# Three norms of a two-layer decoder step: GpSimd instead of VectorE adds blocks 2 to 7 to X

## The reference, cut to what matters

```
def rmsnorm(x, w):
    y = x * rsqrt(mean(x * x, axis=-1) + 1e-6)
    return y * w

def ffn_sublayer(x, pre_w, w_gate, w_up, w_down, post_w):
    h = rmsnorm(x, pre_w)
    y = (silu(h @ w_gate) * (h @ w_up)) @ w_down
    return x + rmsnorm(y, post_w)

# layer 0:  x = x + rmsnorm(even_mixer(rmsnorm(x, mix_pre0)), mix_post0);  x = ffn_sublayer(x, ...)
# layer 1:  x = x + rmsnorm(mamba2_mixer(rmsnorm(x, mix_pre1)), mix_post1);  x = ffn_sublayer(x, ...)
```

## Time and profile before

| what | us |
|---|---|
| median of three runs (lowest, highest) | 1102.64 (1100.86, 1103.34) |
| profiled execution, span from its first to its last instruction | 1097.7 |
| between that span and the median of the runs | 4.9 |
| busy in the span: PE / DVE / ACT / POOL | 1031.3 / 705.6 / 503.3 / 52.9 |
| the nine adds of 128x576 at line 2211, together | 6.8 |

### The profile page before, as it was taken

One profiled execution on the slowest core, in us unless ns is written; L12 is line 12 of the kernel. 1 busy time (PEld: TensorE's weight loads), 2 busy tenths in 40 slices (PEclk: granted clock), 3 DMA queues, 4 the chain that ended last, 5 costly groups with the idle time before them and its releaser, 6 DMA issues.

```text
span 1097.7 us, 21745 instructions
## 1 busy us (share of the span) xinstructions
PE 1031.3 (94%) x8763; PEld 947.1 (86%) x8763; DVE 705.6 (64%) x1296; ACT 503.3 (46%) x902; POOL 52.9 (5%) x97
## 2 busy tenths in 40 slices
PE   8999999888889999999889999889999799999996
PEld 7988888533579999999889999768889799999995
DVE  5644678655448566643498997778984676566343
ACT  5222444232355344343458675554764543444341
POOL 8001300000000000000000000021000000000000
PEclk9999999879898999999989999899999899999998
DMA  9637999999953555455524555089135265554501
GB/s 303 185 99 251 331 348 348 339 348 348 338 173 115 161 180 160 150 168 166 171 78 153 170 177 154 1 281 330 45 121 157 81 189 154 176 169 135 182 30 43
DMA packets 193074, 206.17 MB, mean 188 GB/s; under 512 B 7172, under 2 KB 185561, under 8 KB 192923
## 3 DMA queue, kind: packets, MB, share of 16 engines
q1 hardware_dynamic: 174046, 178.65, 51.6%
q10 hardware_dynamic: 15232, 14.68, 4.2%
q0 software_dynamic: 3696, 11.45, 3.3%
HBM read 192.59 MB, written 12.17 MB: 187 GB/s over the span
## 4 chain that ended last, share of the span: by engine, by line
PE 84%; DVE 7%; DMA 3%; ACT 2%; POOL 1%; issue 1%; SPq 1%; ACTq 0%; POOLq 0%; DVEq 0%
PE acc L822 21%; PE acc L824 21%; PE acc L823 21%; PE trb L915 3%; PE scb L936 3%; PE acc L915 3%; PE scb L1048 2%; PE scb L793 1%; DVE RR L1802 1%; DMA ring<-in_state_ssm_dram 1%; DMA ring<-in_cache_v_dram 1%; SPq L597 1%; DVE X L2211 1%; DVE Y L2210 1%; PE acc L1196 1%
## 5 line engine op out<-in xcount | busy, mean ns | idle before, releaser
L822 PE MATMUL acc<-HX,WHL 128*128 128x288 f32 x928 | 281.0, 303 | 14.8 <-DVE HX L1814 10.2
L823 PE MATMUL acc<-HX,WHL 128*128 128x288 f32 x928 | 277.5, 299 | 0.0
L824 PE MATMUL acc<-HX,WHL 128*128 128x288 f32 x928 | 277.1, 299 | 0.0
L1401 ACT ACTIVATE WHL<-ring 128x1024 fp32r<-128x1024 f32 (+1 forms) x140 | 138.8, 1039 | 200.3 <-PE acc L824 200.3
L1825 DVE TENSOR_TENSOR WHL<-ring,WHL 128x1024 fp32r<-128x1024 f32 (+1 forms) x140 | 163.5, 1208 | 69.5 <-ACT WHL L1401 69.4
L822 PEld LDWEIGHTS acc<-HX,WHL 128*128 128x128 f32 x928 | 178.4, 192 | 18.2 <-issue 12.9
L823 PEld LDWEIGHTS acc<-HX,WHL 128*128 128x128 f32 x928 | 179.9, 194 | 0.2
L824 PEld LDWEIGHTS acc<-HX,WHL 128*128 128x128 f32 x928 | 179.4, 193 | 0.0
L1401 ACT ACTIVATE W<-ring 128x1024 fp32r<-128x1024 f32 x84 | 82.6, 1031 | 130.4 <-PE acc L824 130.4
L1825 DVE TENSOR_TENSOR W<-ring,W 128x1024 fp32r<-128x1024 f32 x84 | 97.1, 1197 | 54.1 <-ACT W L1401 54.1
L822 PE MATMUL acc<-HX,W 128*128 128x288 f32 x352 | 105.7, 300 | 5.5 <-DVE HX L1814 5.1
(11 more groups left out here) (413 smaller groups left out, 1855.3 us busy)
## 6 DMA issues: line engine op xcount, KB each, us to landing
ring<-in_l_w_in_dram SPq DMA_DIRECT2D x32, 1024.0 KB, 5.4
ring<-in_l_ffn_gate_dram SPq DMA_DIRECT2D x22, 1024.0 KB, 5.3
ring<-in_l_ffn_up_dram SPq DMA_DIRECT2D x22, 1024.0 KB, 5.3
ring<-in_l_ffn_down_dram SPq DMA_DIRECT2D x16, 1024.0 KB, 5.1
Z<-in_cache_k_dram SPq DMA_DIRECT2D x52, 256.0 KB, 7.7
ring<-in_cache_k_dram SPq DMA_DIRECT2D x52, 256.0 KB, 7.3
Z<-in_cache_v_dram SPq DMA_DIRECT2D x48, 256.0 KB, 7.1
ring<-in_cache_v_dram SPq DMA_DIRECT2D x48, 256.0 KB, 6.6
```

The costliest lines, as they stand in the source:

```text
L822: pe.matmul(out, w[:, 0, at:at + P], part_at(k, 0), start=(k == 0), stop=False)
L823: pe.matmul(out, w[:, 0, at:at + P], part_at(k, 1), start=False, stop=False)
L824: last = pe.matmul(out, w[:, 1, at:at + P], part_at(k, 0), start=False, stop=(k == kdim - 1))
L1401: act.activation(split_weights(i)[:, 0, half], ring[:, slot_of(u), half], ACT.Copy).then_inc(w_hi, 1)
```

## The change

At the three norms ahead of a projection DVE goes on with multiplying all of Y by RR, and with adding blocks 0 and 1 to X. Blocks 2 to 7 are added by POOL, in three instructions of two blocks each. DVE counts up `y_scaled` when a pair is multiplied, POOL waits for that and counts up `x_later` when a pair is added, and ACT waits for `x_later` before it scales a block from 2 on. DVE doesn't wait behind these multiplies any more. At the last norm everything stays with DVE. The nine adds stand in POOL's program at two places: six behind the stores of the conv rows, three behind the stores of the states.

```
+            def add_later(n):
+                for i, first in enumerate((2, 4, 6)):
+                    pool.wait_ge(y_scaled, 3 * n + i + 1)
+                    pool.tensor_tensor(X[:, first:first + 2, :], X[:, first:first + 2, :], Y[:, first:first + 2, :],
+                                       ALU.add).then_inc(x_later, 1)
...
+            add_later(0)
+            add_later(1)
             pool.wait_ge(acc_full, ACC_SSD)
...
+            add_later(2)
             pool.wait_ge(stored, 16 * stores[0])
...
-            def pre_norm(i, hx, col, x_base):
+            def pre_norm(i, hx, col, n):
                 for k in range(KD):
-                    act.wait_ge(x_made, x_base + k + 1)
+                    if k < 2:
+                        act.wait_ge(x_made, 2 * n + k + 1)
+                    else:
+                        act.wait_ge(x_later, 3 * n + k // 2)
                     scaled(hx, k, col + k)
...
-                    link(dve.tensor_tensor(y, y, RR[:, :].unsqueeze(1).to_broadcast([P, size, NT]), ALU.mult))
-                    dve.tensor_tensor(x, x, y, ALU.add).then_inc(x_made, size)
+                    ins = dve.tensor_tensor(y, y, RR[:, :].unsqueeze(1).to_broadcast([P, size, NT]), ALU.mult)
+                    if hx is not None and first >= 2:
+                        ins.then_inc(y_scaled, 1)
+                    else:
+                        link(ins)
+                        dve.tensor_tensor(x, x, y, ALU.add).then_inc(x_made, size)
```

More of the change, by code:

```diff
@@ L336, in hybrid_decoder_kernel @@
         x_made = sem("x_made")
+        y_scaled = sem("y_scaled")
+        x_later = sem("x_later")
         qz_made = sem("qz_made")
@@ L1353, in _ @@
             for i in range(2):
-                pe.wait_ge(x_made, 3 * KD + 4 * i + 4)
+                pe.wait_ge(x_made, 3 * 2 + 4 * i + 4)
                 for t in range(3):
@@ L1612, in _ @@
             post_norm(N_DOWN0, ACC_DOWN0, 3, PN["ffn_post0"], 1)
-            pre_norm(N_IN1, HX1, PN["mix_pre1"], KD)
+            pre_norm(N_IN1, HX1, PN["mix_pre1"], 1)
             def dt_function(step, dst, src, func, scale=1.0):
@@ L1759, in _ @@
             post_norm(N_OUT1, ACC_OUT1, CX // KD, PN["mix_post1"], 2, input_norm=True)
-            pre_norm(N_GU1, HX2, PN["ffn_pre1"], 2 * KD)
+            pre_norm(N_GU1, HX2, PN["ffn_pre1"], 2)
             hiddens(1, N_GU1, ACC_GU1)
```

## The result

The changed kernel takes 1109.11 us in the median of five runs (1102.23 to 1110.82); the kernel before, run beside it, 1101.61 (1100.25 to 1103.34). The ratio is 1.0068, with a 95% interval of 1.0042 to 1.0093: slower by 7.5 us, where 3.7 were forecast. The profiled execution's span is 1108.3 us against 1097.7. That pair lies further apart than the medians: nearly every timed execution takes 1.7 us more than its own span, so the profiled one of the kernel before took about 1099.4 (an estimate from 1097.7 and 1.7), some 3 us less than its median of 1102.64. Most of the 4.9 us that the table of before puts outside the span is this scatter.

The account below looks back on a forecast made before the run. PE carries 84% of the chain, waiting on DVE at the norms. Losses of 0.55, 1.68 and 1.45 us make 3.7, added to the median 1102.64 for 1106.3 us; range 1101.0 to 1109.5.

Parts of the forecast that it names:

- The two engines take turns: At the norms, DVE and POOL reads of SBUF exclude each other; 3.7 us slower; chance 0.42 with a near 1.2.
- The price of an add, a = 1.2: Each POOL add of two blocks at the norms takes 1.2 us, against 0.76 on DVE; ends 0.76 and 2.03.
- the midway value: a = 1.2 us per POOL add, midway between 0.85 for one stream of 576 and 1.56 for two.
- near 1.2 us of work: Sign of being right: POOL's nine adds at the three norms each show near 1.2 us of work.
- Who comes first: At the norms POOL starts only where DVE has nothing lined up; first add behind the multiply of 4-5, 330.35 to 331.55.
- 1.93: Lateness of DVE's row at a norm in us, L = 3a - 1.67, from three handovers and three slower adds.
- From lateness to PE: At the three norms, DVE lateness beyond the spare time costs PE: 0.55, 1.68 and 1.45 us, together 3.7.
- spare time of 1.38, 0.25 and 0.48: DVE lateness in us that costs PE nothing at the first, second and third norm; all beyond it costs.
- The clock at the norms: Rival: without turns, PE's clock rises sooner at the first two norms, 1 us won each, 1099.4 us; chance 0.10.
- the case without turns: Rival: POOL reads while DVE works at the norms without slowing; together -1.2 us, 1101.4 us; chance 0.24.
- The sum: Losses at the three norms, 0.55, 1.68 and 1.45 us, together 3.7 us, giving 1106.3 us.
- the dearest adds: POOL adds at the norms at a = 1.56 give 1109.5 us, at 2.03 1113.8; later clock or beyond 1.56: chance 0.11.

Follow-up runs that it names:

- writes alone: Kernel before, DVE adding all blocks, with POOL writing a scratch tile three times without reading after each pair at the norms: 1100.87 us, ratio 1.0009.
- dead adds: Kernel before, DVE adding all blocks, with POOL adding 512 columns of a constant into a scratch tile after each pair at the norms: 1109.27 us, ratio 1.0082.
- the last batch: Kernel before and changed kernel, each with about half the first PE fill plus 6 products, beside the kernel before (1099.85 us): 1098.51 and 1099.13 us.
- changed, filled: Changed kernel with 68 small dead products on PE ahead of four waits of the state stage: 1106.67 us, ratio 1.0060 to the kernel before.
- before, half the fill: Kernel before with 5, 14, 4 and 10 dead PE products in the state stage, 6 more ahead of the samples' own scores: 1098.51 us, ratio 0.9980.

## Why the prediction was right in its direction, and where not

*The two engines take turns: right.* POOL's and DVE's reads exclude each other, and DVE's row ends later though it has less to do. Held instructions on DVE in a kernel where no work at the norms waits for POOL show it (1.59 for 0.75), writes alone do not.

*The price of an add, a = 1.2: right, in part by luck.* Freed of its wait it is 1.27 to 1.28; the midway value had no row of an add behind it. "GPSIMD Engine Reference" of the Trainium skill, section on elementwise cycle accounting, had led to an estimate of 1.27, and the trace agrees. The profile's mean of 1.69 is add and wait together, as the first norm's rows show; I had named "near 1.2 us of work" as the mark, and who takes 1.69 for the work would call the step wrong.

*Who comes first: wrong, and this is the step that failed in the norms.* I let POOL start only where DVE had nothing lined up, from one old place (a select of 3.83 us). POOL takes its turn at the end of a DVE instruction, mostly the next one. At the third norm the multiply of 4-5 did come first, as I had it:

```profile
876.80 0.51 DVE L1829 SCALAR_TENSOR_TENSOR HX<-X,par,HX 128x288 fp32r<-128x288 f32 x1
877.23 0.75 DVE L2225 TENSOR_TENSOR Y<-Y,RR 128x576 f32<-128x576 f32 x1
879.86 1.50 DVE L1829 SCALAR_TENSOR_TENSOR HX<-X,par,HX 128x288 fp32r<-128x288 f32 x2 [1.88 <-ACT HX L1404]
881.28 0.75 DVE L2225 TENSOR_TENSOR Y<-Y,RR 128x576 f32<-128x576 f32 x1
881.95 2.11 DVE L1829 SCALAR_TENSOR_TENSOR HX<-X,par,HX 128x288 fp32r<-128x288 f32 x2
```

Blocks 2 and 3 were then late as computed (the rest of block 3 ends 7.39 us behind the first multiply; I had 7.43). But the third add did not wait for the row of multiply and rests to end: it went between the rests of 4 and 5, which is why two of them took 2.11. So the splits were 1.41 to 1.48 us late, not 1.93. In the first norm the earlier turn showed on PE as well: I had its block 2 start 0.84 us later than before, and it starts 0.43 sooner, 3.40 us behind PE's first product instead of 3.83.

```profile
331.08 0.40 PE L834 MATMUL acc<-HX,WHL 128*128 128x288 f32 x1 [0.23 <-DVE HX L1829]
```

*From lateness to PE: right in form.* Less the spare time of 1.38, 0.25 and 0.48, that lateness gives 0.03, 1.16 and 1.00; measured 0.26, 1.08 and 1.23. In the second norm DVE no longer waits for the root, as forecast. PE waited for the sum at all three norms, also at the second, where I had named no such wait: it comes for the sum 15.98 and 15.95 us behind the first multiply in the first two norms, hardly sooner than before (16.05 and 15.97), and the sum is 1.41 late against 1.38 and 1.30 to spare.

*The clock at the norms: a rival had it.* I had tied a sooner rise to the case without turns. It came with turns: from PE's first product on, over the same 7.70 us as in the earlier trace rows, the mean is 0.81 instead of 0.50. This is a tendency, not a rule: over the same 7.70 us the 16 changed norms of the kept profiles have 0.60 to 0.81, but for one of 0.50, and 23 unchanged ones 0.50 to 0.62, but for three of 0.75 to 0.78 (those beside dead adds left out).

```profile
327.68:335.38 7.70, 6.36 (x31) 5.37 (x31) 7.63 (x8) 3.33 (x6) 4.95 (x3) 0.81 0.00 0
```

It won nothing, since DVE's row sets the end there.

*The sum: 3.7 forecast, 2.6 in the norms, and some 5 us that had no term.* The difference of the medians, 7.5, less 2.6 I put down to the state stage's clock: keeping PE on there brings the two kernels to within 0.6 us. The size of 5 is a difference of medians and of one pair of profiles; in that pair itself the stretch is 9.5 us longer. I searched for consequences of the change only where it moved instructions. The kernel before showed the stage's waits and its clock of 0.91 between 700 and 720, and I did not ask what another arrival would make of them. That 1109.11 still lies in the range is luck: the dearest adds had stretched it to 1109.5, and this was not foreseen.

*Open:* why the changed kernel meets more of the lower clock in the state stage, 130 us behind its second norm, and how often each kernel meets it. Any one kernel's times scatter by some 8 us (the kernel before, 1094.7 to 1102.4 in all but two runs of the last batch), and the mean granted clock goes with them (changed kernel: 1102.32 at 0.960, 1113.59 at 0.948). A part of that scatter lies ahead of the first norm, where none of these kernels differs from another: the first norm's first multiply starts at 322.52 us in one profile (changed, filled) and at 329.60 in another (before, half the fill), and from 260 to 320 us their mean clocks are 0.97 and 0.80.

## What to carry to other kernels

Moving adds from VectorE to an idle GpSimd did not free VectorE here, because the two held each other up in reading SBUF. Read the added instruction's duration against the rows of the other engine, since each waits out the other's instruction, and count what the added handovers put on the chain. A small local price can come with a larger one elsewhere: compare the granted clock window by window in stretches that the change doesn't touch before explaining the whole by the change. Filling the holes of TensorE with dead products there, in both kernels, told a clock from a cost here.

## What the runs showed of the hardware

POOL's add of 512 columns of a constant took 1.18 to 1.24 us and held a DVE multiply by 0.84; three writes of the same tile took 1.69 together and held nothing. A product of 64x128 by 128 columns in fp32 cost 0.23 us at the upper clock. Filling the holes of the state stage lifted its granted clock from 0.91 (before) and 0.59 (changed) to 1.00 between 700 and 720 us.
